# Experts' down projection: weight columns as the moving operand instead of activation columns

## What is computed

```python
a = jnp.einsum('becd,edf->becf', xg, lw['w_gate'])
u = jnp.einsum('becd,edf->becf', xg, lw['w_up'])
y = jnp.einsum('becf,efd->becd', jax.nn.silu(a) * u, lw['w_down'])
y = y * gates[..., None].astype(y.dtype)
...
x = x + gate2 * expert_choice_ffn(h, lw)
```

## Time and profile before

| | |
|---|---|
| median of 3 runs | 3066.35 us (3066.34 to 3071.18) |
| the profiled execution: its own time, its span | 3064.96 us, 3063.2 us |
| PE busy | 2932.2 us, 96% |
| PEld busy | 2734.7 us, 89% |
| DVE busy, ACT busy | 1826.4 us (60%), 1663.2 us (54%) |
| mean granted TensorE clock | 0.975 of full |
| matmuls of the experts (L94, L95, L96 into `e_ps`) | 9216 |
| start of expert 0, of expert 15 | 1803.3 us, 2955.8 us |

### The profile page before, as it was taken

How to read it: one execution, slowest core, us unless ns; L and a number is a source line. 1 busy time by engine, 2 the same in 40 slices (tenths; PEclk the granted TensorE clock), 3 DMA queues, 4 the chain that set the end, 5 groups by cost and what they waited for, 6 DMA issues and landing times. The chain is left out here.

```text
span 3063.2 us, 57430 instructions
## 1 busy us (share of the span) xinstructions
PE 2932.2 (96%) x20876; PEld 2734.7 (89%) x20876; DVE 1826.4 (60%) x2958; ACT 1663.2 (54%) x3219; POOL 702.3 (23%) x878
## 2 busy tenths in 40 slices
PE   8999997899999999999899879999999999999996
PEld 5888886789999999999788769999999999999996
DVE  6222224889888888888533576655555555555555
ACT  4222222678888888888444336544444444444444
POOL 1333334642423232332000011111111111111104
PEclk9999999999999999999999779999999999999998
DMA  7212126411010010101364336566666666666657
GB/s 262 79 69 69 68 69 184 161 61 36 17 31 20 17 34 17 34 17 36 106 204 157 103 126 192 186 195 194 195 196 193 195 193 194 195 194 195 194 180 285
DMA packets 320128, 394.74 MB, mean 129 GB/s; under 512 B 30260, under 2 KB 276488, under 8 KB 319016
## 3 DMA queue, kind: packets, MB, share of 16 engines
q1 hardware_dynamic: 307416, 356.18, 35.2%
q0 software_dynamic: 12240, 36.77, 4.9%
q10 hardware_dynamic: 384, 0.62, 0.1%
HBM read 319.60 MB, written 74.06 MB: 129 GB/s over the span
## 5 line engine op out<-in xcount | busy, mean ns | idle before, releaser
L2973 DVE TENSOR_TENSOR e_w_lo<-e_raw,e_w_hi 128x2048 fp32r<-128x2048 f32 x189 | 433.1, 2291 | 412.2 <-ACT e_w_hi L2890 412.2
L94 PE MATMUL e_ps<-e_x_hi,e_w_hi 128*128 128x272 f32 x2048 | 601.5, 294 | 2.7 <-issue 2.6
L96 PE MATMUL e_ps<-e_x_hi,e_w_lo 128*128 128x272 f32 x2048 | 593.3, 290 | 0.0
L95 PE MATMUL e_ps<-e_x_lo,e_w_hi 128*128 128x272 f32 x2048 | 589.9, 288 | 0.0
L1666 ACT ACTIVATE a_pT_hi<-a_ps_t 128x512 fp32r<-128x512 f32 (+1 forms) x640 | 323.7, 535 | 138.5 <-PE a_ps_t L1487 138.1
L1758 DVE TENSOR_REDUCE a_mx<-a_ps_s 128x1 f32<-128x896 f32 (+1 forms) x384 | 349.3, 910 | 68.9 <-PE a_ps_s L1477 58.9
L94 PEld LDWEIGHTS e_ps<-e_x_hi,e_w_hi 128*128 128x128 f32 x2048 | 386.2, 189 | 3.1 <-issue 3.0
L95 PEld LDWEIGHTS e_ps<-e_x_lo,e_w_hi 128*128 128x128 f32 x2048 | 386.9, 189 | 0.0
L96 PEld LDWEIGHTS e_ps<-e_x_hi,e_w_lo 128*128 128x128 f32 x2048 | 385.7, 188 | 0.0
L1783 DVE TENSOR_TENSOR a_pT_lo<-a_ps_t,a_pT_hi 128x512 fp32r<-128x512 f32 (+1 forms) x640 | 365.2, 604 | 26.3 <-ACT a_pT_hi L1666 25.8
L2890 ACT ACTIVATE e_w_hi<-e_raw 128x2048 fp32r<-128x2048 f32 x189 | 360.6, 1908 | 0.0
(11 more groups left out here) (377 smaller groups left out, 5456.4 us busy)
## 6 DMA issues: line engine op xcount, KB each, us to landing
e_raw<-in_w_gate SPq DMA_DIRECT2D x64, 1024.0 KB, 4.9
e_raw<-in_w_up SPq DMA_DIRECT2D x64, 1024.0 KB, 5.0
e_raw<-in_w_down SPq DMA_DIRECT2D x64, 1024.0 KB, 5.0
s_ret<-p_pr SPq DMA_DIRECT2D x17, 768.0 KB, 3.6
p_raw<-in_w_in SPq DMA_DIRECT2D x8, 1152.0 KB, 18.6
o_cT<-s_ct SPq DMA_DIRECT2D x17, 512.0 KB, 4.8
s_x<-o_x SPq DMA_DIRECT2D x17, 512.0 KB, 5.0
s_xn<-o_xn SPq DMA_DIRECT2D x17, 512.0 KB, 3.5
```

The costliest lines, as they stand in the source:

```text
L94: nc.tensor.matmul(out, w_hi, x_hi, start=first, stop=False)
L95: nc.tensor.matmul(out, w_hi, x_lo, start=False, stop=False)
L96: return nc.tensor.matmul(out, w_lo, x_hi, start=False, stop=last)
L2973: nc.vector.tensor_tensor(w_lo[n % RING][:, :, :], raw[n % RING][:, :, :], w_hi[n % RING][:, :, :].bitcast(F32), ALU.subtract).then_inc(w_ ...
```

## The change

Down swaps its operands: the activations `h` are stationary (128 tokens), the weights moving (512 columns, two chunks side by side). A half of the 1024 output columns is three results: latent tokens 0 to 127, latent tokens 128 to 255, each 24 matmuls, and the context tokens. For these, `h_c` holds the high part of the 16 tokens in columns 0 to 15 and the low part in columns 32 to 47 of a 64-column stationary: one matmul with `w_hi` makes two of the three products, a second one with a 16-column stationary and `w_lo` the third; 16 matmuls of 512 columns. DVE adds the two row groups. Token rows come out directly: `turn_sums` is gone; `gate2` is a column factor now, spread over partitions once in expert 0 (`gate_row`, 16 matmuls, kept by ACT).

```diff
-        NP = 3 * FF // P
-        SUMS_AFTER = {0: (0, 1), 1: (2, 3), 2: (4,)}
+        NP = PAIRED + 6
+        GATE_ROW_AFTER = {0: 0, 1: 1, 2: 2, 7: 3}
+        def products_by(m):
+            return 2 * (m + 1) if m < 8 else PAIRED + 3 * (m // 2 - 3)
@@ pool: scatter, two latent pieces and then 16 context rows; the last expert's old rows
+                pool.indirect_dma_start(x1, bass.IndirectOffsetOnAxis(ap=early.row[0:CAP_CTX, e:e + 1] ...), yc, None, compute_op=ALU.add)
@@ tensor
-            def turn_sums(e, q):
...
+            def gate_row(r):
...
+                    ins = nc.tensor.matmul(ps_t[1][:, c * P:(c + 1) * P],
+                                           g["mod"][:, GATE2 + r % 2 * 4 + c, r // 2:r // 2 + 1].broadcast_to([P, P]), g["ident"][:, :],
+            def down_products(e, n):
+                half_at, grp = (n - 8) // 2, n % 2
+                if grp == 0:
+                    pe.wait_ge(w_hi_ok, e * PER + n + 2)
+                    pe.wait_ge(w_lo_ok, e * PER + n + 2)
+                slots = slice(2 * half_at, 2 * half_at + 2)
+                q = PAIRED + 3 * half_at + grp
+                free_bank(e, q)
+                for c in range(FC):
...
+                    ins = three_pass(nc, out, h_hi[:, c, r], h_lo[:, c, r], early.all_hi[:, slots, c, :], early.all_lo[:, slots, c, :],
+                                     c == 0, c == FC - 1)
+                ins.then_inc(mm_done, 1)
+                if grp == 1:
+                    context_products(e, q + 1, slots)
+            def context_products(e, q, slots):
...
+                def context_high(c):
+                    return nc.tensor.matmul(out[0:64, :, :], h_c[:, c, :], early.all_hi[:, slots, c, :], start=(c == 0), stop=(c == FC - 1))
+                context_high(0)
+                for c in (*range(FC - 2), FC - 1, FC - 2):
+                    nc.tensor.matmul(out[0:CAP_CTX, :, :], h_c[:, c, 0:CAP_CTX], early.all_lo[:, slots, c, :],
+                                     start=False, stop=False)
+                    if c != FC - 1:
+                        ins = context_high(c + 1)
+                ins.then_inc(mm_done, 1)
             def free_bank(e, q):
                 if q < BANKS:
                     if not (isinstance(e, int) and e == 0):
-                        pe.wait_ge(yT_ok, (e - 1) * 2 * DC + (q + 2 * DC // 2 - BANKS + 1) * 2)
+                        pe.wait_ge(yg_ok, (e - 1) * SUMS + (q + 2) % BANKS + 1)
@@ scalar: split, the part w_hi of a chunk
-                    act.wait_ge(mm_done, (e * PER + n - RING + 1) * 2)
+                    m = n - RING
+                    act.wait_ge(mm_done, e * NP + products_by(m) if m >= 0 else (e - 1) * NP + products_by(m + PER))
@@ scalar: after h_hi of two blocks; the copies out of down (L2949) are gone
+                        nc.scalar.activation(h_c[:, n - 1:n + 1, 0:CAP_CTX], hT[:, :, CAP:SLOTS], ACT.Copy).then_inc(hc_hi_ok, 1)
@@ vector: sums of a half, called after split at n = 9 and n = 11
-                        for q in SUMS_AFTER.get(n - 1, ()):
-                            sums(e - 1, q)
+                q = PAIRED + 3 * half_at
+                dve.wait_ge(mm_done, e * NP + q + 3)
...
+                nc.vector.tensor_copy(yc[:, part], con[0:CAP_CTX, :]).then_inc(yc_part, 1)
+                scale(0)
+                add_part(1)
+                scale(1)
...
+                    if n == 9 or n == PER - 1 and not last:
+                        sums(e, (n - 8) // 2)
```

More of the change, by code:

```diff
@@ L2609, in experts @@
         hT = k.sb("e_hT", [P, 2, SLOTS])
[L2610 to L2612 removed]
+        h_hi, h_lo = (k.sb(f"e_h_{n}", [P, FC, PITCH], F32R)[:, :, 0:SLOTS] for n in ("hi", "lo"))
+        h_c = k.sb("e_h_c", [P, FC, 64], F32R)
+        gate2 = k.sb("e_gate2", [P, 2, D])
+        yg, yc = k.sb("e_yg", [P, 2, D]), k.sb("e_yc", [P, D])[0:CAP_CTX, :]
+        x1_c = xT[:, :, :].rearrange("p c t -> p (c t)")[0:CAP_CTX, 0:D]
         OWN, NB, LAST = 4, 8, NE - 1
@@ L2876, in _ @@
             over_experts(pe, body)
-            for q in range(SUMS):
-                turn_sums(NE - 1, q)
-                if q == 3:
-                    pe.wait_ge(sq_ok, NTA + 1)
-                    nc.tensor.matmul(ps[0][:, 0:1], early.alike[:, :], ss[:, NTA:NTA + 1], start=True, stop=True).then_inc(ss_c_ok, 1)
         @block.scalar
@@ L2919, in body @@
                 for n in range(PER):
-                    if not (last and n + AHEAD >= PER):
+                    if n < 8:
                         split(e, n + AHEAD)
@@ L2925, in body @@
                         lists.far(act, LIST_IN[e, n])
+                    if isinstance(e, int) and e == 0 and n - 1 in GATE_ROW_AFTER:
+                        keep_gate_row(GATE_ROW_AFTER[n - 1])
+                    if n >= 8 and not (last and n + AHEAD >= PER):
+                        split(e, n + AHEAD)
                     if not last:
@@ new lines, in sums, with gate @@
+                q = PAIRED + 3 * half_at
+                dve.wait_ge(mm_done, e * NP + q + 3)
+                part = slice(half_at * 512, (half_at + 1) * 512)
+                lat, con = [ps[(q + n) % BANKS] for n in range(2)], ps[(q + 2) % BANKS]
+                n_part, n_scaled = e * 4 + half_at * 2, half_at * 3
+                def gate(n, rows):
+                    return g["gates"][0:rows, e, n:n + 1] if isinstance(e, int) else \
+                        g["gates"][0:rows, bass.ds(e, 1), n:n + 1].rearrange("p a n -> p (a n)")
@@ new lines, in add_part, with scale @@
+                def add_part(j):
+                    dve.wait_ge(yc_part, n_part + j)
+                    nc.vector.tensor_tensor(yc[:, part], yc[:, part], con[32 * j:32 * j + CAP_CTX, :], ALU.add).then_inc(yc_part, 1)
+                def scale(n):
+                    nc.vector.scalar_tensor_tensor(out=yg[:, n, part], in0=lat[n][:, :], scalar=gate(n, P), in1=gate2[:, LAT, part],
+                                                   op0=ALU.mult, op1=ALU.mult).then_inc(y_scaled if at_last else yg_ok, 1)
@@ new lines, in sums @@
+                nc.vector.scalar_tensor_tensor(out=yc[:, part], in0=yc[:, part], scalar=gate(2, CAP_CTX), in1=gate2[0:CAP_CTX, CTX, part],
+                                               op0=ALU.mult, op1=ALU.mult).then_inc(y_scaled if at_last else yg_ok, 1)
+                if at_last:
+                    dve.wait_ge(y_scaled, n_scaled + 3)
+                    nc.vector.tensor_tensor(yc[:, part], yc[:, part], x1_c[:, part], ALU.add).then_inc(yg_ok, 1)
+            def mean(i):
+                dve.wait_ge(sq_ok, i + 1)
+                n = CAP_CTX if i == NTA + 2 else P
+                nc.vector.tensor_scalar(ms[0:n, i:i + 1], ss[0:n, i:i + 1], 1.0 / D, EPS, ALU.mult, ALU.add).then_inc(ms_ok, 1)
@@ L3076, in _ @@
             norm(NTA - 1, x1_row[(NTA - 1) % NB])
-            for q in range(SUMS):
-                sums(LAST, q)
-                if q == 3:
-                    mean(NTA)
+            sums(LAST, 1)
+            mean(NTA)
             mean(NTA + 1)
-            norm(NTA, yg_c[:, :])
+            norm(NTA, yg[:, 0, :])
             mean(NTA + 2)
-            norm(NTA + 1, yg[:, 0, :])
-            norm(NTA + 2, yg[:, 1, :])
+            norm(NTA + 1, yg[:, 1, :])
+            norm(NTA + 2, yc)
         blocks.close()
```

210 lines of the change are left out of this document (108 added, 102 removed).

## The result

| | before | changed |
|---|---|---|
| median | 3067.24 us (3066.34 to 3071.18, 4 runs) | 3194.55 us (3189.58 to 3197.53, 4 runs) |
| ratio | | 1.0411, 95% interval 1.0399 to 1.0423 |
| span of the profiled execution | 3063.2 us | 3187.9 us |
| mean granted clock | 0.975 | 0.969 |

A forecast was written before the change was run, and what follows sets the result against it. PE, busy 96% of the span, was taken to bound the kernel. Terms 77.9 - 28.1 + 3.6 + 40.8 + 12.8 - 5.2 = +101.8 us on 3064.96 gave 3166.8 us, range 3138 to 3218 (8 in 10).

The forecast's parts named there:

- Down's products: Down's matmuls on PE: 24.15 us an expert becomes 29.02, +4.87 an expert, +77.9 us for 16.
- Turns back: The 17 turns of down's results on PE go: 1.87 us an expert, -28.1 us in experts 1 to 15.
- Spreading gate2: 16 added matmuls on PE in expert 0, 32 records of 0.112 us: +3.6 us.
- The wait: PE waits 2.8 us for bank 1 at each next expert's start, behind DVE's low part: +40.8 us; none at half boundary.
- nothing is waited for: At the half boundary, next buffers are wanted 14.5 us later and the chain ends by about 10: no wait.
- The clock: Granted clock falls after half of the 15 PE waits, 1.7 us each: +12.8 us (0 to +26).
- The end: Expert 15's additions, 5.8 us, hide behind the norm; the closing chain takes 20 us against 18.5: -5.2 us.
- A: The main forecast for the whole kernel: 3166.8 us, own range 3143 to 3190, chance 0.74.
- rival B: Changing stationary width drains PE, 0.092 us at each of 32 changes an expert: +47, 3214 us; chance 0.12.
- Rival C: The new wait at experts' starts doesn't show; without wait and clock terms 3113 us; chance 0.08.
- Rival D: Narrow context matmuls run beside each other or products around them; at no cost 3051 us, faster than before; chance 0.03.

The follow-up runs named there:

- the first two experiments: Changed kernel with second-half sums ahead of chunk 2's low part on DVE: 3133.43 us; with that low part made twice ahead of the sums: 3239.44 us.
- the one-width kernel: Changed kernel with the low-weight context products on the same 64-column stationary as the high ones: 3192.59 us.
- the first experiment: Changed kernel with the second half's sums moved ahead of the low part of the next expert's chunk 2 on DVE: 3133.43 us.
- the kernel with the context turned: Changed kernel with both DVE moves (sums, list comparison), then context weights stationary and h_c moving, 128 matmuls an expert for 32, result left turned: 3363.51 us.

## Why the forecast held, and where it was short

1. *Down's products*: +4.87 forecast. Down takes 29.31 us against 24.29 before, +5.02. Context products stand 0.231 us apart and not 0.227; for all experts that is 2 us. The bound from the earlier trace rows was misread: a plain fp32 matmul leaves two records (`gate_row`'s 16 matmuls leave 32, the 40 of L311 leave 80), so the seven records are 3.5 matmuls of 0.48 us and say nothing of an fp32r one. And 0.216 us each would make 72 us, not 73.
2. *Turns back*: -1.87 forecast, -1.86 measured between the two kernels without a wait.
3. *Spreading gate2*: 28 gaps within the four groups of L1983's kind are 0.112 us each; 3.6 us, as forecast.
4. *The wait*: 2.85 us between starts, less the usual 0.126, is 2.72 net (2.8 forecast), 2.25 in experts 1 and 2, where list products stand ahead, 39.9 in all (40.8 forecast). Its cause and its one-to-one price are shown by the first two experiments. But the same step held that at the half boundary "nothing is waited for". **That step failed**, in experts 0 and 1. I had followed the chain to the next buffers and forgot who else waits on DVE there: the comparison for the list product of n = 10 stands behind the low part and the sums. From 1886.81 to 1891.19 are 4.38 us where 0.23 is usual: 2 x 4.15 = 8.3 us were lost, and 11.7 came back with the falls of the clock around them.
5. *The clock*: half of 15 waits at 1.7 us was forecast. In experts 3 to 15 of the profiled run it fell in 6 of 13, at 1.25 to 1.51 us each (83.58 to 83.84 against 82.33; the cheaper ones began before the wait had ended); in that of the one-width kernel, with the same waits, in 10 of 13. So runs of one kernel differ here. Experts 0, 1 and 2 had 9.4, 6.8 and 3.4 us of half clock, against 3.0, 0 and 0 before; at 1.5 us for each 3.4 that is 7.3 us, where 1.7 had been put for their two waits. The middle of the term was right for the loop and too small for the first experts, where the clock fell beside the stalls of step 4 too.
6. *The end*: the last `sums` start 89.1 us after the start of expert 15, behind the norm, as forecast. The reason given, that whatever PE gains or loses in expert 15 is hidden behind the norm, holds for down alone: without 30 of the context products they start only 0.4 us earlier (86.02 us after the start of expert 15 against 86.45). The norm's own first square stands on ACT behind a product of expert 15, and so the wait at its start moves it: it begins 45.7 us after that start, and in the first experiment, without a wait, 42.9 us after it (the last `sums` at 86.35); in the kernel before, with turns and no wait, it was 44.7. The turns' -1.87 and the wait's +2.72 pass through and nearly cancel; that the figure came out is in part luck. The -5.2 also gave back expert 15's share of the clock, 0.85, without saying so. What follows takes 23.9 us, and not 20:

```profile
3074.90 0.28 PE L94 MATMUL e_ps<-e_x_hi,e_w_hi 128*128 128x272 f32 x1
...
3120.29 0.40 ACT L2991 ACTIVATE e_act<-e_ps 128x272 f32<-128x272 f32 x1 [2.63 <-PE e_ps L96]
3120.59 1.05 ACT L3010 ACTIVATE f_junk<-f_x 128x1024 bf16<-128x1024 f32 x1
...
3164.02 0.67 DVE L3085 COPY e_yc<-e_ps 16x512 f32<-16x512 f32 x1
...
3176.72 0.84 POOL L2742 DMA_INDIRECT out_y_prompt<-e_yc,f_ctx_row  x1 [0.30 <-issue]
```

From the first `sums` to the last store's issue are 12.7 us against 9.9 in the earlier trace rows: eight DVE instructions in a row where there were five with turns beside them, and a third norm of 1.27 us. Then 11.2 us pass to the end of the span, against 8.6, though the store's last packet ends 2.5 us after its issue, and 3.1 before. The difference is POOL's closing DRAIN, a sequencer instruction that stands in the packed trace and in none of the views: it is recorded with 7.89 us (from 3179.73) against 4.71 before (from 3058.30). It has 7.89 in all seven kernels with the new down and 4.71 in the two with the old one; why stays open.

The 4.0 us ahead of expert 0 are no part of the change: expert 0 starts at 1803.3 in the trace of before, and between 1801.8 and 1807.8 in those of kernels that hardly differ up to there.

Of the 22.9 us that the sum was short: 4.0 ahead of the experts, 14.1 in experts 0 to 2 (8.3 of them the two stalls, most of the rest the clock), 0.7 in experts 3 to 14 and 4.1 in expert 15 and the end. A's own range ended at 3190, below the measured median. The measured time stayed within the range because the range had been stretched towards rival B, not because these terms had been seen.

Rival B (a change of width drains PE) is refuted by the starts and by the one-width kernel. The one fp32 row was the wrong witness for it. The Trainium skill's "PSUM — Partial Sum Buffer", The four PSUM rules, has float32r matmuls forcing the full column group; these traces agree in so far as no drain shows where the width changes (0.231 us from start to start), but the column group itself stands in none of them. Rival C (no wait to be seen) would have been right with the two DVE steps exchanged: 3133 us measured, 3113 worked out without the two stalls, the end and the clock around the stalls. Rival D (narrow products beside each other) is out: the 30 left out gave back 0.232 us each.

## What to carry to other kernels

Count moving columns first: 16 tokens that ride in a 272-column moving operand cost, at 0.463 ns a column, about 1.4 us an expert (an estimate from the earlier trace rows; no run took them out there), and the same 16 as a stationary cost all 512 weight columns each time, 7.4 us measured; a swap of operands that is a gain for full groups can be turned by a remainder group. Then read the order on each engine that empties banks or fills buffers: five instructions put behind one that must wait for the end of the stage cost 40 us and the clock beside it; exchanging the two gave 61 us between the medians, 52 of them in the experts of the profiled executions. When a step is called hidden, list every instruction behind it in its queue, in the unrolled first iterations too, and ask whether the work that is to hide it starts from the same step.

## What the runs showed of the hardware

- The granted clock can fall without any idle time of PE: in the kernel with the context turned it went from 1.00 to 0.50 (2.4 to 1.2 GHz) in the middle of fp32r products of 64 and 16 moving columns, and the 131 us of that kernel that the number of matmuls does not explain go with it. At half clock these products stood 0.213 us apart. What about them brings the fall no run separates.
- The same wait of 2.85 us brought a fall in 6 of 13 experts in one profiled run and in 10 of 13 in another, one of 5.18 us in every one. A fall of 3.4 us cost 1.25 to 1.51 us; the longer wait brought falls of 6.8 us in 8 of 13.
- An fp32r matmul of 128 stationary columns took 0.112 us from start to start with 64 and with 16 moving columns, 0.126 with 272 and 0.227 with 512, at clock 1.00. With 512 moving columns, stationaries of 64 and 16 columns in turn took 0.231.
- POOL's closing DRAIN was recorded with 4.71 us in both kernels with the old end and with 7.89 us in the seven with the new one, after the last store's packets had ended.
